# A decoder layer on one core: prompt attention and the recurrent heads' norm moved into the key stage, the output projection split over input halves, and rows gathered by halves

## What is computed

```
u    = x * (1 + sc1) + sh1                      # adaLN, from silu(c) @ w_ada
proj = u @ w_in                                 # hq hf hi hg (recurrent), sq sk sv (attention), 8 heads each
o_h  = rms_norm(hgrn2(hq, hf, hi), hg_norm) * silu(hg)
o_s  = rms_norm(stick_breaking(sq, sk, sv, bias), sb_norm)
       # z = q.k / sqrt(128) + bias ; a = exp(logsig(z) + sum of log(1 - sig) over later keys) ; o = a @ v
       # sample tokens also attend to two cached pages of 128 keys each, found by a page table
mix  = concat(o_h, o_s) @ w_o
x    = layer_norm(ALPHA * x + g1 * mix)
u2   = x * (1 + sc2) + sh2
y    = layer_norm(ALPHA * x + g2 * moe(u2))     # 4 groups of 8 experts; best group, 2 experts in it
```

## Time and profile before

| | us |
|---|---|
| median of three runs | 1879.05 |
| lowest, highest | 1875.29, 1883.8 |
| the profiled execution, its own time | 1882.17 |
| its span, first to last instruction | 1880.4 |
| PE busy in the span | 1638.4 (87%) |
| DVE, ACT, POOL busy | 541.3, 176.5, 123.8 |
| moved by DMA | 536.86 MB, mean 286 GB/s |

### The profile page before, as it was taken

How to read it: one execution, slowest core, us unless ns; L and a number is a source line. 1 busy time by engine, 2 the same in 40 slices (tenths; PEclk the granted TensorE clock), 3 DMA queues, 4 the chain that set the end, 5 groups by cost and what they waited for, 6 DMA issues and landing times.

```text
span 1880.4 us, 24737 instructions
## 1 busy us (share of the span) xinstructions
PE 1638.4 (87%) x9575; PEld 989.2 (53%) x9575; DVE 541.3 (29%) x894; ACT 176.5 (9%) x270; POOL 123.8 (7%) x153
## 2 busy tenths in 40 slices
PE   3679999999999999769987999998988898989871
PEld 0046666446787844547763565554545454545440
DVE  0010029712212222540026222313131313232328
ACT  0000011100000010330005100000000000000002
POOL 3000000001101100020011000000000000000004
PEclk8689999999979899679997799999999999999995
DMA  9998878874424255143342599999999999999951
GB/s 355 421 384 316 311 314 331 318 285 148 148 91 135 97 203 186 57 192 134 112 157 96 197 415 408 404 422 421 410 399 415 396 415 403 410 417 420 413 216 50
DMA packets 78909, 536.86 MB, mean 286 GB/s; under 512 B 10202, under 2 KB 10378, under 8 KB 17370
## 3 DMA queue, kind: packets, MB, share of 16 engines
q1 hardware_dynamic: 72146, 507.62, 67.9%
q0 software_dynamic: 6384, 26.28, 4.5%
q10 hardware_dynamic: 336, 2.36, 0.3%
HBM read 532.87 MB, written 11.80 MB: 290 GB/s over the span
## 4 chain that ended last, share of the span: by engine, by line
DMA 29%; PE 21%; DVE 4%; issue 1%; SPq 1%; ACT 1%; DVEq 0%; ACTq 0%
DMA ring<-w_up 29%; PE ps L886 7%; PE ps L1010 7%; PE ps L1029 2%; SPq L356 1%; PE ps L992 1%; PE ps L900 1%; ACT arena L1219 0%; DVE arena L1631 0%; PE ps L964 0%; PE ps L878 0%; PE ps L877 0%; DVE arena L1759 0%; DVE bnst L1806 0%; PE ps L910 0%
## 5 line engine op out<-in xcount | busy, mean ns | idle before, releaser
L1010 PE MATMUL ps<-ring,arena 128*64 128x256 f32 x3200 | 365.9, 383 | 26.8 <-DMA ring<-w_up 23.7
L1010 PEld LDWEIGHTS ps<-ring,arena 128*64 128x64 f32 x3200 | 256.1, 138 | 141.7 <-DMA ring<-w_up 49.3
L579 PE MATMUL ps<-arena,ring 128*128 128x288 f32 x1280 | 322.7, 411 | 0.0
L579 PEld LDWEIGHTS ps<-arena,ring 128*128 128x128 f32 x1280 | 241.5, 191 | 89.8 <-issue 25.2
L1029 PE MATMUL ps<-arena 128*64 128x512 f32 x800 | 177.2, 595 | 23.5 <-DVE arena L1770 23.5
L563 PE MATMUL ps<-ring,silu_c 128*32 128x512 f32 x768 | 115.7, 713 | 54.2 <-DMA ring<-w_ada 29.0
L886 PE MATMUL ps<-arena,ring 128*128 128x288 f32 x512 | 128.3, 410 | 11.2 <-DVE arena L1599 11.2
L992 PE MATMUL ps<-arena 64*128 64x512 f32 x400 | 109.8, 634 | 24.4 <-DVE arena L1759 15.1
L1029 PEld LDWEIGHTS ps<-arena 128*64 128x64 f32 x800 | 66.1, 137 | 118.5 <-issue 90.4
L886 PEld LDWEIGHTS ps<-arena,ring 128*128 128x128 f32 x512 | 98.4, 192 | 39.0 <-DVE arena L1599 11.7
L1766 DVE TENSOR_TENSOR arena<-arena,ps 128x256 f32<-128x256 f32 x25 | 10.5, 422 | 370.1 <-PE ps L1010 370.1
(11 more groups left out here) (389 smaller groups left out, 1261.4 us busy)
## 6 DMA issues: line engine op xcount, KB each, us to landing
ring<-w_gate SPq DMA_DIRECT2D x100, 1024.0 KB, 26.3
ring<-w_up SPq DMA_DIRECT2D x100, 1024.0 KB, 28.1
arena<-w_down SPq DMA_DIRECT2D x100, 1024.0 KB, 21.9
ring<-w_ada SPq DMA_DIRECT2D x96, 1024.0 KB, 8.2
ring<-w_in SPq DMA_DIRECT2D x56, 1024.0 KB, 6.3
ring<-w_o SPq DMA_DIRECT2D x16, 1024.0 KB, 5.1
ring<-cache_k SPq DMA_DIRECT2D x16, 512.0 KB, 4.3
ring<-cache_v SPq DMA_DIRECT2D x16, 512.0 KB, 4.1
```

The lines of the kernel that those rows point to most:

```text
L579: last = mm(ps[:, bank, 0:T], ring[:, slot, P * t:P * (t + 1)], uT[:, t, :], start=(t == 0), stop=(t == KC - 1))
L1010: last = mm(ps[B * s:B * (s + 1), 2 + c // 4, 0:256], xgT[:, 4 * (c % 4) + t, :], ring[:, c, 512 * t + 256 * s:512 * t + 256 * (s + 1)], s ...
```

## The change

Three edits go together.

1. Prompt attention goes into the key stage, one head a round. In round c PE forms head c's scores first, turns the first key page, does half of the row chunk, turns the second page into the same two PSUM banks, does the rest, then the running sums. The recurrent head c is squared by ACT (`hsq`), summed by a product with ones into the bank of the scores, and normalised by DVE, in the same round. The attention weights of all heads are kept (`aa`, eight tiles), and their products with the values come after the stage, in two groups of four. The first-page copies and the score scaling of the sample tokens move accordingly.
2. The output projection runs over the recurrent heads first (half 0: sixteen tiles of eight products each), with the value products, the sample attention and the attention heads' norm between its first tiles, and then over the attention heads (half 1). Half 0 is parked in `rsT` and the input is added there. The sums for the LayerNorm are no longer products with ones for each tile: DVE adds up values in `mu` and squares in `lt1`, and one product each adds over partitions at the end. The output weights come as 32 loads of 512 KB. POOL's squaring and scaling go away, and its load of `xT` waits only for the new keys' scores.
3. A gather brings 128 half rows of 4 KB instead of 64 rows of 8 KB. The slots are permuted over partitions by `iotap` (the value at column 32a + 4b + c is 32a + b + 8c), PE turns eight pieces of 128 x 128, and ACT's copy puts the halves in place.

The diff, cut to its core:

```diff
         uT = area(0, KC, T)
-        mixT = uT
+        mixT = hf_hq
...
+        aa = area(TOK + 3072, H, 384)
+        hsq, hrs = area(TMP + 8192, T), area(TMP + 8192 + T, T)
...
+        def wo_of(half, m):
+            pair = 8 * half + m // 2
+            return N_V + (pair if pair == 0 else pair + 8)
...
+            def put_wo(half, m):
+                n = wo_of(half, m)
+                sp.wait_ge(ring_used, used(n - SLOTS))
+                for k in range(2):
+                    sp.dma_start(ring[:, n % SLOTS, 1024 * k:1024 * (k + 1)],
+                                 w_o[(m + k) // SLOTS, (m + k) % SLOTS][:, 1024 * half:1024 * (half + 1)]
+                                 ).then_inc(slot_loaded[n % SLOTS], 16)
...
+            put_wo(0, 0)
             for b in range(NSEQ):
-                put_pages(N_V + b, b, cache_v)
+                put_pages(page_of(b), b, cache_v)
+            for m in range(2, 2 * KC, 2):
+                put_wo(m // KC, m % KC)
...
-            nc.gpsimd.tensor_tensor(sqo[0], hout, hout, ALU.mult).then_inc(nsq_pool, 1)
...
-            nc.gpsimd.tensor_scalar(xa, xa, ALPHA, 0.0, ALU.mult, ALU.add).then_inc(xa_ready, 1)
...
+            for c in range(SLOTS):
+                n, nr = N_SV + 2 * c, N_SV + 2 * c + 1
+                if c == 0:
+                    pe.wait_ge(kout_evac, 2)
+                else:
+                    pe.wait_ge(hrs_act, c)
+                z = ps[:, 2, :]
+                mm(z[:, 0:256], skT[:, c, 0:128], sqT[:, c, 0:256], start=True, stop=True)
+                mm(z[:, 256:384], skT[:, c, 128:256], sqT[:, c, 128:256], start=True, stop=True).then_inc(z_pe, 1)
+                pe.wait_ge(slot_loaded[n % SLOTS], loaded(n))
...
+                turn_page(n % SLOTS, 0).then_inc(kT_pe, 1)
...
+                row_steps(nr % SLOTS, c, (0, 1))
+                pe.wait_ge(kT_act, c + 1)
+                turn_page(n % SLOTS, 1).then_inc(ring_used, 1)
+                if c >= 1:
+                    turn_scores(c - 1)
+                row_steps(nr % SLOTS, c, (2, 3))
+                sample_steps(nr % SLOTS, c)
+                pe.wait_ge(sp_ready, c + 1)
...
+                mm(s[:, 256:384], tri[:], spl[:, 256:384], start=True, stop=True).then_inc(c_pe, 1)
+                pe.wait_ge(z_dve, c + 1)
+                pe.wait_ge(hsq_act, c + 1)
+                mm(ps[:, 2, 0:T], ones[:], hsq, start=True, stop=True).then_inc(hrms_pe, 1)
+                pe.wait_ge(kT_dve, c + 1)
...
+            project(0, 0)
+            attend(range(4))
...
+            project(0, 4)
+            head_squares(0)
+            project(0, 5)
+            project(0, 6)
+            head_squares(1)
+            for m in range(7, KC):
+                project(0, m)
...
+            for m in range(KC):
+                project(1, m)
...
-                if m >= 2:
-                    sums(m - 2)
-            sums(KC - 2)
-            sums(KC - 1)
...
+                act.wait_ge(d_dve, c + 1)
+                A(aa[:, c, :], zn, ACT.Exp).then_inc(a_ready, 1)
+                act.wait_ge(hrms_pe, c + 1)
+                if c >= 1:
+                    act.wait_ge(hnorm_dve, c)
+                link(A(hrs, ps[:, 2, 0:T], ACT.Ln, bias=epsr[:, 0:1], scale=1.0 / P))
+                A(hrs, hrs, ACT.Exp, scale=-0.5).then_inc(hrs_act, 1)
...
+            for m in range(3, KC):
+                project_half(m)
+                if m in (7, 9):
+                    norm_heads((m - 7) // 2)
+            dve.wait_ge(xa_loaded, 16)
+            dve.wait_ge(wo_half, KC)
             for m in range(KC):
-                dve.wait_ge(ring_used, used(N_WO + m))
+                add_input(m)
...
+                v.tensor_tensor(rsT[:, m, TP:T], rsT[:, m, TP:T], samp2, ALU.add).then_inc(wo_dve, 1)
+                if m >= 1:
+                    add_square(m - 1)
...
+                    v.tensor_tensor(mu, mu, rsT[:, m, :], ALU.add).then_inc(lsum_dve, 1)
...
-                nc.gpsimd.indirect_dma_start(out=xg, out_offset=None, in_=u2_rows[:],
+                nc.gpsimd.indirect_dma_start(out=xg, out_offset=None,
+                                             in_=u2_rows.rearrange("t (h n) -> (t h) n", h=2),
...
-                for m in range(KC):
-                    last = nc.tensor.transpose(ps[:, m // 8, B * (m % 8):B * (m % 8 + 1)], xg[:, P * m:P * (m + 1)],
-                                               ident[0:B, 0:B])
+                for m in range(KC // 2):
+                    last = nc.tensor.transpose(ps[:, m // 4, P * (m % 4):P * (m % 4 + 1)], xg[:, P * m:P * (m + 1)],
+                                               ident[:])
```

More of the change, by code:

```diff
@@ L581, in head_chunk, with row_steps @@
                 last.then_inc(ring_used, 1)
-            def row_chunk(slot, c):
-                for t in range(4):
+            def row_steps(slot, c, steps):
+                for t in steps:
                     for i, (t0, tn) in enumerate(TILES[:2]):
@@ new lines, in _, with project @@
+            turn_scores(NSEQ - 1)
+            def project(half, m):
+                n = wo_of(half, m)
+                pe.wait_ge(slot_loaded[n % SLOTS], loaded(n))
+                if half == 0:
+                    pe.wait_ge(hnorm_dve, H)
+                    bank = 2 + m % 2
+                    if m >= 2:
+                        pe.wait_ge(wo_half, m - 1)
+                else:
+                    bank = 4 + m % 4
+                    if m >= 4:
+                        pe.wait_ge(wo_dve, m - 3)
+                for k in range(H):
+                    at = 1024 * (m % 2) + P * k
+                    last = mm(ps[:, bank, 0:T], ring[:, n % SLOTS, at:at + P], mixT[:, H * half + k, :],
+                              start=(k == 0), stop=(k == H - 1))
+                last.then_inc(ring_used, 1)
@@ L857, in _ @@
-            pe.wait_ge(d_dve, H)
-            pe.wait_ge(o_evac, H)
-            pe.wait_ge(ss_dve, 5)
-            for n in range(4):
-                group, half = n // 2, n % 2
-                if group == 0:
-                    pe.wait_ge(nsq_pool, 1)
-                else:
-                    pe.wait_ge(nsq_act, half + 1)
-                    pe.wait_ge(nln_act, n - 1)
+                        last = mm(ps[32 * j:32 * j + 32, i, 0:P], apad[:, pg, b, k, :],
+                                  ring[:, n % SLOTS, 1024 * pg + P * k:1024 * pg + P * (k + 1)],
+                                  start=(b == 0 and pg == 0), stop=False)
@@ new lines, in _ @@
+                last.then_inc(ring_used, 1)
+            for k in range(H):
+                i, j = k // 4, k % 4
+                last = mm(ps[32 * j:32 * j + 32, i, 0:P], aN[:, k, :], tok[0:TS, 2, P * k:P * (k + 1)],
+                          start=False, stop=True)
+            last.then_inc(ss_pe, 1)
+            project(0, 2)
+            pe.wait_ge(ss_dve, 4)
+            for i in range(2):
+                last = nc.tensor.transpose(ps[:, 0, P * i:P * (i + 1)], orow[:, i, :], ident[:])
@@ L947, in _ @@
                 for i in range(3):
-                    last = mm(ps[0:B, 4, 0:NB1], rsel[k][:, i, :], bsel[k][:, i, :],
-                              start=(k == 0 and i == 0), stop=(k == 1 and i == 2))
+                    for h in range(2):
+                        last = mm(ps[B * h:B * (h + 1), 4, 0:NB1], rsel[k][:, i, :], bsel[k][:, i, :],
+                                  start=(k == 0 and i == 0), stop=(k == 1 and i == 2))
             last.then_inc(rt_pe, 1)
@@ new lines, in _, with copy_heads @@
+                A(hrs, hrs, ACT.Exp, scale=-0.5).then_inc(hrs_act, 1)
+            def copy_heads(heads):
+                for k in heads:
+                    act.wait_ge(o_pe, k + 1)
+                    nc.scalar.copy(mixT[:, H + k, 0:TP], ps[:, 6 + k % 2, 0:TP]).then_inc(o_evac, 1)
+            act.wait_ge(ss_dve, 1)
+            A(eP, zP, ACT.Abs)
+            link(A(eN, zN, ACT.Abs))
+            A(eP, eP, ACT.Exp, scale=-1.0)
+            link(A(eN, eN, ACT.Exp, scale=-1.0))
+            A(eP, eP, ACT.Ln, bias=1.0)
@@ L1185, in _ @@
+            for half in range(2):
+                heads = slice(4 * half, 4 * half + 4)
+                act.wait_ge(nm_pe, half + 1)
+                A(rst[:, heads, :], ps[:, 4:8, 0:T], ACT.Ln, bias=epsr[:, 0:1], scale=1.0 / P).then_inc(nln_act, 1)
+                act.wait_ge(nln_act, half + 1)
+                A(rst[:, heads, :], rst[:, heads, :], ACT.Exp, scale=-0.5).then_inc(nrs_act, 1)
             for m in range(KC):
```

543 lines of the change are left out of this document (252 added, 291 removed).

## The result

The changed kernel takes **1797.58 us** (median of four runs, 1795.09 to 1799.18), against 1878.78 for the kernel before on the same chip: a ratio of **0.9565**, 95% interval 0.954 to 0.9589. The profiled execution took 1795.09 us, its span is 1793.3, and it is the one read here.

The account below looks back on a forecast made before the run. PE bounds the kernel ahead of expert block 0, DMA weight transfers behind it. Attention -57.0, index step and gathered rows' turns +0.5, gather -12: -68.5 us, on the median of 1879.05 a forecast of 1811 us, range 1798 to 1834.

Parts of the forecast that it names:

- rival (d): Expert stream: PE reaches block 0 earlier, but expert 0's weights or the plan are late; 1867 us, chance 0.04.
- the attention part: From 657.6 us to the end of the first LayerNorm's sums: 264.4 us against 321.4, 57.0 less.
- the waits at the ends of heads: Key stage: PE waits for ACT to read the norm's sums in bank 2; 0.85 us, seven times, 5.9.
- head 4's: Key stage: head 4's scores wait while DVE adds the sample rows in head 3; 1.2 us.
- The seam: Between key stage and projection: 22.6 us of PE work and about 2.0 us of waits.
- The tail: End of the projection: two remaining sum products with the last evacuation, square and add; 3.0 us.
- Rival (b): Between key stage and projection: half the work at 1.2 GHz costs some 11 us; 1822 us, chance 0.15.
- Rival (c): Key stage: waits of 0.85 us a head keep the clock at 1.2 GHz; 104.5 us more, 1915, chance 0.04.
- the part in the stream: Expert blocks: half-row gathers in spread order recover somewhat over half of the rate's loss; 12 us less.
- Rival (a): Expert stream: the gather change gains nothing; 1822.5 us, chance 0.15.
- (e): Expert stream: the gather gains all its loss, with no other change; 1803 us, chance 0.10.
- the bound: Expert stream: most the gather could gain, from a mean 410 instead of 421 GB/s over 24 blocks; 19.6 us.

Follow-up runs that it names:

- the run without the cover: Changed kernel with the three products of the running sum directly behind a head's scores, so no other PE work hides the DVE and ACT chain; 1845.18 us.
- bad order: Changed kernel gathering 64 whole rows, eight consecutive slots put into partitions p to p+3 and p+32 to p+35; 1832.94 us.
- fillers: Changed kernel plus products that nothing reads: 23 while PE waits for the LayerNorm, one behind each of twelve token turns; 1796.06 us.

## Why the prediction was off, point by point

**Right: what bounds the kernel and what moves it.** PE ahead of block 0, the transfers behind it; rival (d), a stream that does not start earlier, did not happen, since block 0 came 59.4 us earlier and the stream with it. "PE is waiting for weights" says too much, though: the 27 us of the earlier trace rows are a transfer under way, and in such a block PE is busy 27.7 of 30.2 us.

**Right, term by term: the attention part,** -54.9 for -57.0 in the trace and 55.7 us by the kernel with the old gather. The key stage ends at 772.1 us, forecast 770.2: the heads' PE work is 13.53 us (14.11 less 0.58), not 13.06, 3.8 us more over eight; the waits at the ends of heads are 0.58 instead of 0.85 and head 4's 0.83 instead of 1.2, 2.3 less. The seam without its seven half projections takes 24.7 us to 824 (51.9 less 7 x 3.88), forecast 22.6 + 2.0. The tail is 3.0, as forecast. Rival (b), half clock in the seam, did not happen: 1.00 in all three windows. Rival (c) did not either: 1.00 over the key stage with twenty transposes a head, and the run without the cover shows what kind of wait it takes. By the rule of the Trainium skill weighed there ("TensorE: Matmul & The Clock Gate", "Part 4: PE-mode transpose": transposes do not count) the stage was at risk; the trace does not agree.

**Wrong: the part in the stream,** 12 us with a bound of 19.6, measured 24.2 in the trace, 25.1 alone on the kernel before, and 26.6 in the medians when undone. Rival (a), no gain, did not happen; (e), all the loss gone, is what came, but it was priced at the bound, 1803, and the bound was too low. The step that failed is the sentence "If pieces of half the size halve the largest share, somewhat over half goes; I take 12 us", with two faults. Both show in what moved between the starts of blocks 1 and 24 (the last column, a mean over the last block: a chunk's landing is recorded in sixteen parts, and this is the time from the first to the last of them):

| gather | us | MB moved | GB/s | first to last part, us |
|---|---|---|---|---|
| kernel before: whole rows, slot order | 713.7 | 293.45 | 411 | 16.4 |
| changed kernel: whole rows, slot order | 712.9 | 293.18 | 411 | 16.6 |
| the same, permuted order | 708.7 | 291.40 | 411 | 9.9 |
| the same, bad order | 728.0 | 294.29 | 404 | 17.5 |
| changed kernel: half rows, slot order | 693.1 | 291.67 | 421 | 12.6 |
| the same, permuted order (the change) | 689.4 | 290.09 | 421 | 4.6 |

The first fault is the part of the rate's loss that goes. With half rows the rate is 421 GB/s in either order: all of the loss is gone, not somewhat over half. 293.45 MB at 421 instead of 411 GB/s are some 16 of the 24.2 us. The prediction put the loss down to uneven shares of the engines; most of it was that all packets became slow while whole rows came in, which half rows do not do.

The second fault is the bound: a mean rate does not show all that uneven shares cost. At the start of block 24 the kernel before had moved 3.36 MB more, with no more of the blocks done: some parts of the stream ran ahead of others, up to 16 us at the end, and PE can start on a chunk only when its last part has landed. 3.36 MB at 421 GB/s are the other 8 us. This part goes with the order too: half rows in slot order move at the same rate as in permuted order, but 1.58 MB more, which is 3.8 us for the 3.6 measured.

What the place of a row does shows in how long a gather lasts. 5 rows last 1.1 us in slot order, 0.6 in permuted order and 2.4 in the bad one, 30 rows 2.0, 2.1 and 3.9; in slot order 33 rows last 2.0 us and 36 rows 3.3 to 3.7. That goes by the fullest group of eight partitions, four neighbours and the four that lie 32 further on: 4, 1 and 5 rows in the first case, 4, 4 and 8 in the second, 5 and 8 in the third. Why packets become slow with whole rows stays open. It is not the order, and not how long the gather lasts: half rows in slot order take as long to come in (3.4 us for 36 rows), and no weight packet behind block 1's start takes over 0.4 us. But half rows go to 128 partitions and whole ones to 64, and no run parts the size of the piece from the number of partitions. Which engine moved a packet is in no trace here either.

The groups of eight stand in the Trainium skill, "DMA: Bandwidth & Descriptors", section "The descriptor swizzle": in a transfer to 128 partitions engines 0 to 7 write partitions 0 to 63 and engines 8 to 15 the others, four neighbours at a time, repeating after 32. The lengths of the gathers agree with these groups; that one engine serves a group here is not shown. The prediction weighed another section of that page, by which 64 rows use all sixteen engines. With sixteen packets under way in the gathers too, the trace does not speak against that section; what the prediction drew from it, that halving gives nothing, did not come out.

**Not forecast: the router stage and block 0,** -7.5 us in the profiled pair. It is clock. Windows of the kernel before, the last two ahead of block 0, and of the kernel after:

```profile
1040.00:1048.00 8.00, 7.98 (x32) 4.64 (x30) 3.60 (x3) 3.52 (x5) 1.16 (x2) 0.50 0.22 55
1048.00:1056.00 8.00, 6.06 (x26) 4.43 (x27) 1.36 (x1) 0.00 (x0) 0.18 (x1) 0.50 0.04 14
```

```profile
977.00:989.00 12.00, 12.00 (x46) 5.26 (x45) 8.21 (x24) 4.75 (x8) 1.47 (x3) 0.50 0.13 44
989.00:994.30 5.30, 3.35 (x23) 2.76 (x22) 1.36 (x1) 0.71 (x1) 1.23 (x2) 0.99 0.14 36
```

Before, half clock reaches into block 0; after, it ends 5 us ahead of it. In the thirteen profiles the two together, from the router's first product to block 1, take 76.2 to 78.3 us six times and 81.3 to 84.1 seven times. The six all have half rows; so have three of the seven, one of them with the changed kernel's router code to the letter (the norm's sum in bank 0: 81.9). So it is not fixed by that code. Whether the gather has a hand in it, and what else sets it, stays open; fillers did not hold the clock.

With the measured 24.2 in its place the prediction's own sum is -57.0 + 0.5 - 24.2 = -80.7, 1798.4 on the median, for 1797.58 measured. So close a meeting is in part luck: in the profiled pair the attention part gave 2.1 us less than forecast, and the router stage and block 0 gave 7.5 that no term held.

## What to carry to other kernels

A gather's price in a stream that fills the DMA engines is not its bytes alone. Look for slices in which the rate falls while the engines stay busy, and for how long single packets take there; here half rows over 128 partitions in place of whole rows over 64 removed that, and spreading the rows over groups of partitions came second. A mean rate does not price uneven loads: compare the bytes moved by the same point of the program, or how far apart the parts of one chunk land. And ask what bounds next: here the 29.4 us that PE needs for a block were at most 3.6 us below the period, before the change. A chain through three engines put under a row of products is worth its wait and the clock that PE would lose behind it: here 3 us a head net on paper, 6 measured.

## What was not expected of the hardware

The recurrent stage, which the change does not touch, has two lengths: from the product of L746 at 536.6 us to the first turn of L771 it took 117.0 to 117.1 us in ten of the thirteen profiles (before and after among them) and 111.5 in three. Windows of the kernel with half rows in plain order and of the changed kernel, its last stretch:

```profile
620.00:647.20 27.20, 26.67 (x153) 21.83 (x153) 6.22 (x10) 0.99 (x2) 1.69 (x2) 0.93 0.35 107
```

```profile
620.00:653.70 33.70, 33.29 (x165) 27.82 (x163) 6.22 (x10) 0.98 (x2) 2.89 (x3) 0.81 0.31 100
```

The difference shows as clock, 0.93 against 0.81; what sets it is not shown. This stage and the router stage with block 0 together come to 192.8 to 201.2 us in the thirteen profiles, a difference of 8.4, and nine runs of the kernel before, unchanged, range from 1873.1 to 1883.5 us. That is more than several of the differences measured here, so single profiles can part by as much, medians over few runs by some of it, and stages were compared in their own windows.
